# Expert rows asked for four units ahead instead of eight, and spread over 122 units, beside the second weights of a sparse feed-forward layer

## The reference, cut to what matters

```python
idx = ...                                  # 128 experts of each token
gate = jax.nn.softmax(top, axis=-1)...
u_e = jnp.take(u, idx, axis=0)
v_e = jnp.take(v, idx, axis=0)
act = jax.nn.gelu(jnp.einsum('ted,td->te', u_e, xc).astype(jnp.float32))
return jnp.einsum('te,ted->td', (gate * act).astype(v_e.dtype), v_e)
```

## Time and profile before

| | us |
|---|---|
| median of three executions (2042.24 to 2047.25) | 2044.0 |
| the profiled execution | 2042.94 |
| its span in the trace | 2041.0 |
| second-weights stage, layer 0, first to last matmul at L1101 | 573.5 to 876.1 |
| second-weights stage, layer 1 | 1373.0 to 1676.5 |

### The profile page before, as it was taken

One profiled execution on the slowest core, in us unless ns is written; L12 is line 12 of the kernel. 1 busy time (PEld: TensorE's weight loads), 2 busy tenths in 40 slices (PEclk: granted clock), 3 DMA queues, 4 the chain that ended last, 5 costly groups with the idle time before them and its releaser, 6 DMA issues.

```text
span 2041.0 us, 32925 instructions
## 1 busy us (share of the span) xinstructions
PE 1980.8 (97%) x13084; PEld 1832.4 (90%) x13084; DVE 1378.0 (68%) x2724; ACT 733.2 (36%) x1636; POOL 424.7 (21%) x389
## 2 busy tenths in 40 slices
PE   9999999999999999989999999999999999999999
PEld 9877899999999888977699999999989998778887
DVE  7566679777854544458849977784544647877885
ACT  3455410365510000037541145540102106765554
POOL 1000103555521112110101365552121410000000
PEclk9999999999999999999999999999999999999999
DMA  7536678899999999924467999999999974334664
GB/s 266 195 126 227 237 263 312 356 420 406 393 419 421 421 420 417 381 79 141 158 247 265 345 420 412 396 405 420 421 419 416 410 300 147 105 124 145 189 194 164
DMA packets 110807, 612.38 MB, mean 300 GB/s; under 512 B 13488, under 2 KB 13600, under 8 KB 58432
## 3 DMA queue, kind: packets, MB, share of 16 engines
q1 hardware_dynamic: 70848, 391.61, 50.8%
q0 software_dynamic: 38384, 217.27, 26.4%
q10 hardware_dynamic: 1424, 1.41, 0.2%
HBM read 606.89 MB, written 1.05 MB: 298 GB/s over the span
## 4 chain that ended last, share of the span: by engine, by line
PE 82%; DMA 11%; DVE 4%; ACT 1%; issue 1%; POOL 0%; ACTq 0%; DVEq 0%; POOLq 0%
PE ps L1070 28%; PE ps L1101 19%; DMA plain<-in_peer_v 10%; PE ps L773 5%; PE ps L809 4%; PE ps L812 4%; PE ps L816 4%; PE ps L856 4%; PE ps L776 3%; PE ps L1056 2%; PE ps L845 2%; PE ps L908 1%; PE ps L756 1%; PE ps L759 1%; PE ps L762 1%
## 5 line engine op out<-in xcount | busy, mean ns | idle before, releaser
L1101 PE MATMUL ps<-big,plain 128*128 128x160 f32 x2752 | 388.2, 302 | 21.2 <-DMA plain<-in_peer_v 21.0
L1101 PEld LDWEIGHTS ps<-big,plain 128*128 128x128 f32 x2752 | 378.9, 191 | 28.3 <-issue 21.5
L2209 DVE TENSOR_TENSOR lo<-raw,hi 128x1024 fp32r<-128x1024 f32 (+1 forms) x195 | 236.2, 1219 | 109.4 <-ACT hi L1586 108.9
L1070 PE MATMUL ps<-big,plain 128*128 128x160 f32 x2112 | 302.0, 301 | 3.0 <-issue 2.9
L2618 DVE CUSTOM_DVE_ANT_0 big<-big 128x1024 f32<-128x1024 f32 x152 | 185.1, 1223 | 168.9 <-DMA big<-in_peer_uv,big 166.8
L1070 PEld LDWEIGHTS ps<-big,plain 128*128 128x128 f32 x2112 | 290.8, 191 | 3.7 <-issue 3.7
L2638 DVE SCALAR_TENSOR_TENSOR big<-big 128x1024 f32<-128x1024 f32 x160 | 205.2, 1283 | 120.7 <-DMA big<-in_peer_vr,big 67.7
L1586 ACT ACTIVATE hi<-raw 128x1024 fp32r<-128x1024 f32 (+1 forms) x195 | 204.8, 1055 | 154.7 <-PE ps L816 51.9
L3321 POOL DMA_INDIRECT big<-in_peer_uv,big x122 | 142.9, 1172 | 413.0 <-DVE big L2638 331.5
L1070 PE MATMUL ps<-big,plain_in_xs 128*128 128x160 f32 x1344 | 195.8, 303 | 3.1 <-issue 3.1
L1773 ACT ACTIVATE big<-big 128x1 f32<-128x1 f32 x150 | 30.1, 201 | 462.6 <-DVE big L2618 462.5
(11 more groups left out here) (416 smaller groups left out, 2898.0 us busy)
## 6 DMA issues: line engine op xcount, KB each, us to landing
plain<-in_peer_v SPq DMA_DIRECT2D x86, 1024.0 KB
plain<-in_peer_u SPq DMA_DIRECT2D x66, 1024.0 KB
plain_in_xs<-in_peer_u SPq DMA_DIRECT2D x42, 1024.0 KB
plain_in_xs<-in_peer_v SPq DMA_DIRECT2D x42, 1024.0 KB
big<-in_peer_u SPq DMA_DIRECT2D x20, 1024.0 KB, 7.5
raw<-in_ret_vg SPq DMA_DIRECT2D x32, 512.0 KB, 4.2
raw<-in_peer_q SPq DMA_DIRECT2D x24, 512.0 KB, 5.2
raw<-in_ffn_up SPq DMA_DIRECT2D x22, 512.0 KB, 3.6
```

The source lines that it names most:

```text
L1070: ins = e.matmul(u.view[:, j * DENSE:(j + 1) * DENSE], w[:, k, :], Peer.xT[:, k, :], start=k == 0, stop=k == 7)
L1101: ins = e.matmul(us[b // 2].view[:, b % 2 * DENSE:(b % 2 + 1) * DENSE], w[:, b * 128:(b + 1) * 128], experts[:, k, :], start=k == 0 and b ...
L2209: e.tensor_tensor(ul[:, 0:w], raw[:, i % N_RAW, 0:w], uh[:, 0:w].bitcast(F32), ALU.subtract).then_inc(s_lo, 1)
```

## The change

```diff
-EARLY, RAW_UNTIL = 21, 50
+EARLY, RAW_UNTIL, LAST = 21, 50, 122
...
     for k in range(128):
         looks[k] = []
-        if rest and k % 7 != 6:
+        for m, w in rest[(k * len(rest) + LAST - 1) // LAST:((k + 1) * len(rest) + LAST - 1) // LAST]:
             looks[k].append(len(events))
-            unit.setdefault(rest[0][0], k)
-            events.append(rest.pop(0))
-    assert not rest and len(events) == 2 * LISTS
+            unit.setdefault(m, k)
+            events.append((m, w))
+    assert len(events) == 2 * LISTS
...
-LEAD = 8
+LEAD = 4
```

## The result

| | before | after |
|---|---|---|
| median, us | 2046.32 (2042.24 to 2050.87, 9 runs) | 2051.11 (2048.12 to 2053.63, 9 runs) |
| ratio to before | | 1.0024, 95% interval 1.0016 to 1.0033 |
| profiled execution, us | 2042.94, span 2041.0 | 2048.12, span 2046.0 |
| stage of the second weights, layer 0, us | 573.48 to 875.82: 302.3 | 573.58 to 878.72: 305.1 |
| the same, layer 1, us | 1373.01 to 1676.26: 303.3 | 1376.54 to 1681.34: 304.8 |

A stage is counted from the start of its first L1101 matmul to the start of its last. The change costs 0.24%: small, less than the 0.3% that the prediction called no change, but the interval excludes 1, and 2051.11 us lies above the predicted range. (Part of that height is the measurement: the kernel before stands at 2046.32 here and at 2044.0 in the three runs the prediction had.

What follows compares the result with a forecast made beforehand. The stage was taken as bound by DMA bytes at about 422 GB/s, TensorE close behind. Layer 0 +1 and layer 1 -2 us on the profiled 2042.94 gave 2041.9, as a median 2043.0 us; range 2037 to 2049.

Steps and rivals of the forecast that it cites:

- the new wait: Stage start: row 58 waits until TensorE has done three units, some 6 us; cost 0, weights take the DMA's time.
- layer 1's gain: End of layer 1's stage: weights end last, rows pushed behind them win time; 2 us earlier, bounds 4.2 earlier, 1 later.
- core sentence: Whole stage: while both queues have work the DMA is never idle; moving a row in time removes no bytes.
- Layer 0's end: End of layer 0's stage: gain taken back by late last loads; 1 us later, bounds 2.9 earlier, 6 later.
- SP's hold: Layer 0's end: SP issues in order, so weight loads behind a raw load await the third split; held some 6 and 2 us.
- The third split: Layer 0's end, VectorE's split of raw weights: one sum's cadence earlier (3.7 us), sums 5 later; net 1.3 us later.
- slower rival: Layer 0's end: SP held by the third split, long TensorE wait, clock falls, layer 1 pays 1; 7.7 us, 2051.7; chance 0.10.
- The clock: TensorE after a long wait: costs 1.6 us more than the wait; left at 0, bounds 1.6 each way per layer.
- The lead's size: Each layer, rows pushed back against weights: TensorE gains 1 us by unit 95 (0 to 2.5), 2 by 119 (0 to 4.2).
- The spread: Whole stage: 103 steps over 122 units instead of six in seven; rows lag 1.7 us, cost 0 by itself.
- The count of waits: GpSimd in the stages: waits on TensorE grow from 23 to over 30, those on rooms fall.
- windows below 400 GB/s before 855 us: Refuting sign: DMA below 400 GB/s before 855 us means bytes really were delayed; expected 410 to 424 until 861 us.

Runs made afterwards that it cites:

- e4: The kernel before, with rows 58 to 62 alone asked for four units ahead instead of eight; ratio to before 1.0016.
- e3: The changed kernel, with rows 58 to 62 asked for eight units ahead as before and later rows four; ratio to before 1.0004.
- e6: The changed kernel with the edits of e3 and e5 together; ratio to before 1.0002.
- e5: The changed kernel, with layer 0's last raw-weight load behind weight load 127 instead of 124; ratio to before 1.0015.
- e1: The changed kernel with the old lead of eight units, so the even spread alone; ratio to before 0.9994.
- e7: e1 with layer 0's last raw-weight load moved behind weight load 127; ratio to before 0.9990.
- e8: The kernel before, with layer 0's last raw-weight load moved behind weight load 127; ratio to before 0.9997.
- e12: e7 with a lead of twelve units instead of eight; ratio to before 0.9999.
- e2: The kernel before with the lead cut from eight units to four, old spacing kept; ratio to before 1.0017.
- e9: The changed kernel with a lead of six units instead of four; ratio to before 1.0005.
- e10: e1 with rows from 96 on asked for four units ahead, all earlier ones eight; ratio to before 1.0006.
- e11: e1 with rows 63 to 95 asked for four units ahead, the others eight; ratio to before 1.0011.

## Why the prediction was wrong

**The step that failed first** is the one on the new wait: "Cost 0: the weights take the DMA's time meanwhile." The wait came as described, 574.04 to 580.53 us, 6.5 us for "some 6". But the weights' queue is paced by TensorE, 241 GB/s here, and did not issue one load sooner. The missing bytes, 0.92 and 0.79 MB, are 4.1 us of DMA time; e4 shows five such rows alone costing 3.3, and giving them their lead back gains 0.0020 (e3) and 0.0013 (e6 against e5), 4 and 3 us. The term was put at 0 and is most of the 5 us. The second term that was mis-sized is layer 1's gain: 2 us in the forecast, nothing that a run shows. The prediction's core sentence (moving a row moves bytes past each other "while both queues have work") was right with its condition; at the stage's start the condition doesn't hold. The trace of before could have told it: SP's issues there stand 4.35 us apart.

**Layer 0's end**, forecast 1 us later, is 2.9 later. By its bytes the start's loss is 2.2 of this, but the profiles of layer 0 do not show it so. They go by the lead of the rows from 63 on: the five kernels that keep all rows eight or more ahead (before, e1, e7, e8, e12) took 301.0 to 303.2 us there, the five with four from row 63 on 304.0 to 305.1, whether the start was full (e3, e6) or not (after, e2, e5). e4, with the loss at the start alone, took 303.5. In layer 1 it is the start that shows: 304.8 to 306.5 us with it short, 303.0 to 304.2 with it full, but for e8's 305.0 (e9, with lead 6, 304.8). So it seems that the short lead of the later rows costs some 2 us in layer 0 by itself, where I had a gain that is taken back and 1 us on top. One profile for each kernel, those of e3 and e6 the slowest of their executions, does not prove it, and the cause stays open beyond SP's hold.

**SP's hold.** The third split was to come 1.3 us later and came 3.1 later. The slower rival named this place, and the argument against it, that "the DMA doesn't idle while SP is held", was wrong: 325 GB/s. Yet e5 shows that the hold was only part of the price: of a wait of 5.49 us 0.6 came back in the stage's length (1.8 by the ratios, with intervals that overlap), because the rows then ended last. The rival's chain stood (SP held, TensorE ahead, one wait over 3.6 us, the clock down), its 7.7 us did not: the change costs 5.0 us of span, most of it from another cause. That its 2051.7 lies beside the measured median 2051.11 is luck, since the kernel before stood 2.3 us higher in the same measurement.

**Layer 1**, forecast 2 us earlier, took 1.5 us longer. With the start's 1.9 taken off, 0.4 are left of the gain, less than one profile can show. The last sum did move, from 286.7 us behind the stage's start to 293.6, so the rows were pushed back; in e2 and e5 too (295.4 and 294.4), and none of the three stages is under 304.8 us. "The weights end last, and rows pushed behind them are time won" would hold only if the rows had room behind the weights. In the changed kernel the last sum began at 1670.18 us, after TensorE's last wait for weights, so it seems that both queues shared the DMA to the end. No run pushes back the late rows of layer 1 with a full start, so the step is refuted for the change as it stands and not by itself.

**The clock** was left at 0, with bounds of 1.6 us. In layer 0 the one new long wait put 2.0 us on its next 16 matmuls (4.38 us instead of 2.34). The wait that the prediction read its 1.6 from shrank, from 3.57 us to 2.10, and the 32 matmuls behind it took 6.26 us, 6.25 before: the shorter wait gave nothing of the clock back.

**The lead's size.** I took 1 us by unit 95, with a bound of 2.5, and 2 by unit 119, with 4.2; in layer 0 TensorE was 5.8 us ahead at unit 96, in spite of the megabyte lost. (Some 2 us of this may be scatter: e1 was 2.1 ahead there and e8, the same as before up to this place, 1.5.) The surplus of weights was real and worth nothing, in keeping with the core sentence. **The spread** at cost 0 was right within 2 us (e1). **The count of waits** was right: 33 and 17. The statement that windows below 400 GB/s before 855 us would refute the forecast did its work, though the first such window stood at 579 us, not at the end.

**What stays open.** 0.6 us between the two stages. And the middle and late rows: e3 and e1 differ by 0.001, 2 us, which is the rows from 63 on. e10 and e11, each on e1 with one part of them, stand 0.0012 and 0.0017 above it, together more than the whole, with intervals of 0.001 either way. The bytes that they lose are enough for this (e10 1.9 us at its own jump, which the change has not, and 1.6 from 850 to 855 us; e11 1.1), so that nothing more than this and noise is shown.

## What to carry to other kernels

In a stage bound by bytes, a later request is free only where the other queue can take its place: look at what paces that queue (here the buffers that TensorE frees), and compute its GB/s alone. A cut in the lead, at the stage's start or within it, empties the queue where it makes the gap between two requests longer than the outstanding ones last, and does nothing where the requests were waiting for room anyway; read it in GB/s, since the DMA's busy share stays near 1. And a wait that is removed at a stage's end is worth only the distance to the next stream that ends there.

## What I had not expected

The busy share of the DMA engines hardly shows an idle queue: 328 GB/s at a share of 0.94, 333 at 0.99, where the kernel before has 419 at 1.02 and 424 at 1.03. The loss of bytes has an edge, not a slope: lead 6 keeps 416 GB/s over 573 to 600 us, lead 4 384. And TensorE tells nothing of the loss when it happens: it is full in all these windows, and its waits for weights up to 700 us sum to 3.4 us in e4 and after, 3.1 before. The price comes later in the stage. It isn't the long wait at layer 0's end, though: e4, with the loss, has no wait over 0.64 us there, and e3, without it, one of 6.50.
